# A mixer stage and a feed-forward stage that multiply before their RMSNorm is finished

## What is computed

```python
def rmsnorm(x, g):
    y = x32 * lax.rsqrt(jnp.mean(x32 * x32, axis=-1, keepdims=True) + EPS)
    return (y * g.astype(jnp.float32)).astype(x.dtype)
def modulate(h, shift, scale):
    return h * (1.0 + scale[:, None, :]) + shift[:, None, :]
...
h = modulate(rmsnorm(x, norm_g[l, 0]), sh1, sc1)
x = x + 0.5 * g1[:, None, :] * swiglu(h, w_ffn1_in[l], w_ffn1_out[l])
h = modulate(rmsnorm(x, norm_g[l, 1]), sh2, sc2)
hq, hf_f, hf_b, hi, hg, aq, ak, av = split_columns(h @ w_mix_in[l])
...
x = x + g2[:, None, :] * mixed
h = modulate(rmsnorm(x, norm_g[l, 2]), sh3, sc3)
x = x + 0.5 * g3[:, None, :] * swiglu(h, w_ffn2_in[l], w_ffn2_out[l])
```

## Time and profile before

| | us |
|---|---|
| median of 3 runs (1137.01 to 1138.49) | 1138.09 |
| the profiled execution's own time | 1136.99 |
| its span, first to last instruction | 1135.2 |
| PE busy | 1089.5 (96% of the span) |
| DVE busy | 535.4 (47%) |
| ACT busy | 417.4 (37%) |
| POOL busy | 2.9 (0%) |

### The profile page before, as it was taken

How to read it: one execution, slowest core, us unless ns; L and a number is a source line. 1 busy time by engine, 2 the same in 40 slices (tenths; PEclk the granted TensorE clock), 3 DMA queues, 4 the chain that set the end, 5 groups by cost and what they waited for, 6 DMA issues and landing times.

```text
span 1135.2 us, 12546 instructions
## 1 busy us (share of the span) xinstructions
PE 1089.5 (96%) x5023; PEld 879.4 (77%) x5023; DVE 535.4 (47%) x607; ACT 417.4 (37%) x498; POOL 2.9 (0%) x14
## 2 busy tenths in 40 slices
PE   7699999999999989999998999979999999999998
PEld 4488888888888878778885778758888888888886
DVE  5854545454454574335449984455223222232323
ACT  4542333333232243225247874225333243232321
POOL 0000000000000000000000000000000000000000
PEclk9899999999999989999999999899999999999999
DMA  8855554644355424222310001122332323323212
GB/s 338 298 186 182 189 202 167 220 154 180 125 209 189 133 61 137 95 74 74 111 38 1 2 1 38 37 75 75 111 100 84 111 76 109 108 78 111 79 69 74
DMA packets 89480, 133.46 MB, mean 118 GB/s; under 512 B 10569, under 2 KB 73413, under 8 KB 89318
## 3 DMA queue, kind: packets, MB, share of 16 engines
q1 hardware_dynamic: 89208, 130.82, 33.7%
q10 hardware_dynamic: 238, 2.17, 0.5%
HBM read 128.78 MB, written 4.19 MB: 117 GB/s over the span
## 4 chain that ended last, share of the span: by engine, by line
PE 88%; DVE 6%; ACT 3%; issue 2%; SPq 0%; DMA 0%; POOL 0%; ACTq 0%; DVEq 0%; POOLq 0%
PE bank L1191 27%; PE bank L1193 26%; PE bank L1192 26%; PE bank L1499 1%; PE bank L1229 1%; PE bank L1254 1%; DVE a_diag L1099 1%; DVE qp_both L1082 1%; DVE rinv L854 1%; DVE z L1082 1%; PE bank L1482 1%; PE bank L1217 1%; ACT kc L704 0%; PE bank L1536 0%; DVE lg L1057 0%
## 5 line engine op out<-in xcount | busy, mean ns | idle before, releaser
L1191 PE MATMUL bank<-h_hi,w_hi 128*128 128x512 f32 x976 | 385.2, 395 | 18.8 <-DVE h_lo L865 17.5
L1193 PE MATMUL bank<-h_hi,w_lo 128*128 128x512 f32 x976 | 382.9, 392 | 0.0
L1192 PE MATMUL bank<-h_lo,w_hi 128*128 128x512 f32 x976 | 382.9, 392 | 0.0
L789 DVE TENSOR_TENSOR w_lo<-w_raw,w_hi 128x2048 fp32r<-128x2048 f32 x83 | 190.3, 2292 | 331.0 <-ACT w_hi L524 331.0
L524 ACT ACTIVATE w_hi<-w_raw 128x2048 fp32r<-128x2048 f32 x83 | 158.9, 1915 | 459.8 <-PE bank L1193 459.8
L1191 PEld LDWEIGHTS bank<-h_hi,w_hi 128*128 128x128 f32 x976 | 185.5, 190 | 62.1 <-issue 11.8
L1193 PEld LDWEIGHTS bank<-h_hi,w_lo 128*128 128x128 f32 x976 | 185.1, 190 | 39.3
L1192 PEld LDWEIGHTS bank<-h_lo,w_hi 128*128 128x128 f32 x976 | 185.7, 190 | 38.2
L1191 PE MATMUL bank<-a_hi,w_hi 128*128 128x512 f32 x352 | 137.3, 390 | 0.0
L1193 PE MATMUL bank<-a_hi,w_lo 128*128 128x512 f32 x352 | 137.0, 389 | 0.0
L1192 PE MATMUL bank<-a_lo,w_hi 128*128 128x512 f32 x352 | 137.0, 389 | 0.0
(11 more groups left out here) (161 smaller groups left out, 755.6 us busy)
## 6 DMA issues: line engine op xcount, KB each, us to landing
w_raw<-in_w_ffn_in SPq DMA_DIRECT2D x44, 1024.0 KB, 5.1
ada<-in_w_ada SPq DMA_DIRECT2D x30, 1024.0 KB, 4.9
w_raw<-in_w_ffn_out SPq DMA_DIRECT2D x22, 1024.0 KB, 4.8
w_raw<-in_w_mix_in SPq DMA_DIRECT2D x11, 1024.0 KB, 5.0
ada_first<-in_w_ada SPq DMA_DIRECT2D x6, 1024.0 KB, 17.8
x_nat<-in_x SPq DMA_DIRECT2D x1, 2048.0 KB, 15.4
bias_shear<-rowpad ACTq DMA_DIRECT2D x1, 2048.0 KB, 9.6
w_raw<-in_w_mix_in SPq DMA_DIRECT2D x8, 256.0 KB, 4.4
```

Source lines behind the costliest of these rows:

```text
L789: ve.tensor_tensor(w_lo[n % 2][:], raw[n % 2][:], as_f32(w_hi[n % 2][:]), ALU.subtract).then_inc(wlo_done, 1)
L1191: te.matmul(out_ap, wh, xh, start=first, stop=False)
L1192: te.matmul(out_ap, wh, xl, start=False, stop=False)
L1193: return te.matmul(out_ap, wl, xh, start=False, stop=last)
```

## The change

For the norms r = 1 (in front of the mixer) and r = 2 (in front of the second block) the first stage behind the norm no longer takes `h`. It takes u = `xT * fac`, which needs only the residual. Since h = u·rinv + shift, W·h = (W·u)·rinv + W·shift: the per-token factor `rinv` and the per-output-channel bias W·shift come in when the stage's banks are evicted (`norm_evict`, `wbias`). The parts:

- ACT makes u's high part (`norm_scaled`) and the square of each updated tile; DVE makes u's low part (`norm_ulo`). PE's new `stage_u` waits for `ulo` tile by tile. In it, behind four of eight channel tiles, stands one `ones` matmul for the sum of squares.
- POOL adds up all eight squares in a chain of seven, makes every second `tmod` tile in two steps (times `fac`, times `rinv`), and forms W·shift: the raw weights times the shift (128x2048), three halving adds, and then two one-column matmuls on PE.
- The second stage behind the norm takes `h` as before, through `stage_h`, tile by tile. At the first boundary u and h share memory, so ACT's `h_hi` tile waits for PE to have used that tile of u (`used`).
- In the output projection the two halves of a stage are completed one after the other, and the first half's residual tile is updated in mid-stage (`mx_out`). Banks move: the halves of stage 46 + m go to banks 6 and 7, or 4 and 5.
- The last two modulation vectors come behind m = 1 and m = 2 as eight transposes each (`ada_sum`), in place of the sixteen one-column products in the gap. ACT loads the root's table ahead (`load_sqrt`). The first pair of the second block is taken out of its loop on ACT, DVE and SP.

```diff
+            def weight_bias(nm):
...
+                nc.gpsimd.tensor_tensor(nm.prod[:], raw[n % 2][:].rearrange("p (k m) -> p k m", k=DT), shift, ALU.mult
+                                        ).then_inc(nm.wacc, 1)
+                for i, w in enumerate((4, 2, 1)):
+                    pool.wait_ge(nm.wacc, i + 1)
+                    nc.gpsimd.tensor_tensor(nm.prod[:, 0:w, :], nm.prod[:, 0:w, :], nm.prod[:, w:2 * w, :], ALU.add
+                                            ).then_inc(nm.wacc, 1)
+            def norm_pool(nm):
+                for q in range(1, DT):
+                    pool.wait_ge(nm.sq, q + 1)
...
+                    nc.gpsimd.tensor_tensor(sq[:, d, :], sq[:, d, :], sq[:, before, :], ALU.add).then_inc(nm.acc, 1)
+                for i, q in enumerate(range(1, DT, 2)):
+                    nc.gpsimd.tensor_scalar(tmod[:, d, :], xT[:, d, :], fac[:, nm.r, d:d + 1], None, ALU.mult
+                                            ).then_inc(nm.tp, 1)
+                pool.wait_ge(nm.rinv, 1)
...
+                    nc.gpsimd.tensor_tensor(tmod[:, d, :], tmod[:, d, :], rinv[:], ALU.mult).then_inc(nm.tp, 1)
@@ ACT @@
+            def norm_scaled(nm, q):
+                a.wait_ge(x_upd[nm.r - 1], q + 1)
...
+                sc.activation(nm.u_hi[:, d, :], xT[:, d, :], ACT.Copy, scale=fac[:, nm.r, d:d + 1]).then_inc(nm.uhi, 1)
...
+                    if nm.r == 1 and q < DT - 1:
+                        a.wait_ge(nm.used, q + 1)
+                    elif nm.r == 1:
+                        a.wait_ge(stage_done, N_MIXIN + 1)
...
             ffn_act(ffns[0], False)
-            norm_stats(norms[1])
+            load_sqrt()
+            for q in range(DT):
+                norm_u(norms[1], q)
+            whi(N_MIXIN + 1)
+            norm_root(norms[1])
             norm_hi(norms[1])
-            whi(N_MIXIN + 1)
@@ DVE @@
+            def norm_ulo(nm, q):
+                v.wait_ge(nm.uhi, q + 1)
+                d = nm.order[q]
+                ve.scalar_tensor_tensor(nm.u_lo[:, d, :], xT[:, d, :], fac[:, nm.r, d:d + 1],
+                                        as_f32(nm.u_hi[:, d, :]), ALU.mult, ALU.subtract).then_inc(nm.ulo, 1)
             def norm_dve(nm):
                 norm_root(nm)
+                norm_t(nm, nm.order[0])
+                norm_t(nm, nm.order[2])
+                for q in range(DT):
+                    norm_lo(nm, q)
+                    if q % 2 and q + 3 < DT:
+                        norm_t(nm, nm.order[q + 3])
+            def norm_evict(nm, outs):
+                v.wait_ge(nm.wsum, 1)
+                ve.tensor_copy(wbias[:, nm.r - 1, :], nm.wbank[:, 0:2]).then_inc(nm.ev, 1)
+                for cc in range(2):
+                    ve.tensor_tensor(outs[cc], bank[cc][:], rinv[:], ALU.mult).then_inc(nm.ev, 1)
...
             for m in range(M_MIXOUT):
+                for cc in range(2):
+                    d = 2 * m + cc
+                    if cc == 0:
+                        v.wait_ge(mx_out, m + 1)
+                    else:
+                        v.wait_ge(stage_done, N_MIXOUT + m + 1)
+                    ve.scalar_tensor_tensor(xT[:, d, :], bank[6 - 2 * (m % 2) + cc][:], gates[:, 1, d:d + 1],
+                                            xT[:, d, :], ALU.mult, ALU.add).then_inc(x_upd[1], 1)
+                    if m == M_MIXOUT - 1:
+                        norm_ulo(norms[2], d)
@@ PE @@
+            def stage_u(s, banks, nm):
+                for q, k in enumerate(nm.order):
+                    pe.wait_ge(nm.ulo, q + 1)
+                    for cc in range(2):
+                        col = k * 2 * P + cc * P
+                        ins = three(banks[cc][:], w_hi[s][:, col:col + P], w_lo[s][:, col:col + P],
+                                    nm.u_hi[:, k, :], nm.u_lo[:, k, :], q == 0, q == DT - 1)
+                    if nm.r == 1 and q < DT - 1:
+                        ins.then_inc(nm.used, 1)
+                    if q == 3:
+                        pe.wait_ge(nm.acc, DT - 1)
+                        te.matmul(nm.bank[:], ones[:], sq[:, nm.order[DT - 1], :], start=True, stop=True
+                                  ).then_inc(nm.ss, 1)
+                ins.then_inc(stage_done, 1)
+                pe.wait_ge(nm.wacc, 4)
+                for cc in range(2):
+                    ins = te.matmul(nm.wbank[:, cc:cc + 1], nm.prod[:, 0, cc * P:(cc + 1) * P], ones[:, 0:1],
+                                    start=True, stop=True)
+                ins.then_inc(nm.wsum, 1)
...
+                if m == 0:
+                    stage_u(n % 2, banks, norms[1])
+                elif m == 1:
+                    pe.wait_ge(x_upd[0], DT)
+                    stage_h(n % 2, banks, norms[1])
+                    ada_sum(7, ada_acc2[:, 0], 6)
+                else:
+                    stage_k8(n % 2, banks)
```

More of the change, by code:

```diff
@@ L589, in silu @@
                     sc.activation(sil[:, 1, :], bank[1][:], ACT.Silu).then_inc(f.silu, 1)
-                with a.Fori(0, FPAIRS - 1) as i:
+                first = 0
+                if f.r:
+                    nm, first = norms[f.r], 1
+                    whi(f.n0 + 2, 0)
+                    for cc in range(2):
+                        a.wait_ge(nm.ev, cc + 2)
+                        ins = sc.activation(sil[:, cc, :], sil[:, cc, :], ACT.Silu, bias=wbias[:, 1, cc:cc + 1])
+                    ins.then_inc(f.silu, 1)
+                    whi(f.n0 + 3, 0)
+                with a.Fori(first, FPAIRS - 1) as i:
                     whi(f.n0 + 2, 2 * i)
@@ L1193, in three, with stage_k8 @@
                 return te.matmul(out_ap, wl, xh, start=False, stop=last)
[L1195 to L1206 removed]
+            def stage_k8(s, banks):
+                for cc in range(2):
+                    for k in range(DT):
+                        col = k * 2 * P + cc * P
+                        ins = three(banks[cc][:], w_hi[s][:, col:col + P], w_lo[s][:, col:col + P],
+                                    h_hi[:, k, :], h_lo[:, k, :], k == 0, k == DT - 1)
+                ins.then_inc(stage_done, 1)
@@ L1311, in out_stage @@
                             ins.then_inc(f.out, 1)
-                        if last and q >= 3:
+                        if last and q >= 3 and between:
                             between(q - 3)
@@ L1320, in ffn_pe @@
                 out_stage(FPAIRS - 1, 0, last=True)
[L1321 to L1330 removed]
+                if between:
+                    for q in range(DT - 3, DT):
+                        between(q)
+            ffn_pe(ffns[0], True, None)
+            pe.wait_ge(x_upd[0], 6)
             for m in range(M_MIXIN):
@@ L1356, in _ @@
                     pe.wait_ge(av_cp, 1)
+                    pe.wait_ge(ada_out, 9)
                     if m == 5:
@@ L1513, in _, with out_part @@
             ins.then_inc(oh_ss, 1)
-            def out_part(m, tiles):
+            def out_part(m, tiles, halves=range(2)):
                 s = (N_MIXOUT + m) % 2
-                for cc in range(2):
+                for cc in halves:
                     for k in tiles:
```

269 lines of the change are left out of this document (157 added, 112 removed).

## The result

| | before | changed |
|---|---|---|
| median of the runs, us | 1138.11 (1137.01 to 1138.49) | 1129.65 (1127.93 to 1130.75) |
| span of the profiled execution | 1135.2 | 1126.1 |
| DVE busy | 535.4 | 561.0 |
| ACT busy | 417.4 | 400.4 |
| POOL busy | 2.9 | 75.6 |

What follows compares the result with a forecast made beforehand. PE was taken to bound the kernel, with 88% of the chain. Gains of 9.4 us at the first boundary and 10.8 at the second sum to 20.2, taking 1136.99 to 1116.8, as a median 1118, range 1115.5 to 1133.5.

Steps and rivals of the forecast that it cites:

- stage 33 would follow stage 32 at once: First boundary: PE has no pause after stage 32, its half clock goes, and stage 33 ends at 422.54.
- W·shift in time: First boundary: POOL's product and halving adds take 10.2 us and end by 399, before the first square.
- POOL's add: Both boundaries: one POOL add of 128x512 taken as 1.36 us, between bounds of 0.68 and 1.36.
- The second boundary up to the reciprocal: Second boundary: stage 49 ends at 754.4, the sum starts at 759.8, the reciprocal runs 761.7 to 765.0.
- POOL's four `tmod` tiles run beside: First boundary, stage 34: PE needs no more waits, as DVE's twelve instructions take 8.0 us for 10.88 of PE.
- the case without exclusion: Both boundaries: POOL and DVE do not block each other to any weight; chance 0.50, own range 1115.5 to 1121.
- Stage 33 to stage 34: First boundary: stage 33 starts at 410.72, first `h_lo` is done at 424.1, PE waits 0.9 us from 423.1.
- Stage 34: First boundary: after the 0.9 us wait in front of it, PE needs no more waits inside this stage.
- Stage 35: First boundary: its weights come at 436.1, PE waits 0.3 us; stage 36 can start at 447.8.
- Second boundary: From the end of stage 49 to stage 53: PE waits 0.6 us before stage 51; gain 10.8 us.
- the right rival: Both boundaries: POOL blocks DVE instructions with two SBUF inputs; gain 5.1 us, time 1133 at 1.36 each; chance 0.33.
- Slower than before: Both boundaries: the same blocking with POOL instructions over 1.6 us; at 1.82 each the time is 1146; chance 0.07.

Runs made afterwards that it cites:

- experiment 2: The change with all eight `tmod` tiles on DVE, none on POOL: 1125.33 us, ratio 0.9892 to the kernel before.
- experiment 8: The changed kernel itself, run once more without an edit: 1130.27 us, ratio 0.9936 to the kernel before.
- 5: The change with the adds of squares and all `tmod` tiles on DVE, POOL keeping only W·shift: 1126.02 us, ratio 0.9896.
- 7: The change with `fac` products on ACT and POOL's `rinv` products held back until the first `h_lo` tile: 1129.54 us, ratio 0.993.
- 6: Experiment 2's kernel; at the first boundary POOL adds only five times, DVE once, PE sums two tiles: 1125.65 us, ratio 0.9897.
- 9: Experiment 2's kernel; ACT splits stage 35's weights straight behind its last `h_hi`, DVE's two small tables stand behind `w_lo`: 1124.61 us, ratio 0.9876.
- experiment 3: The change with the `fac` products on ACT, the `rinv` products staying on POOL: 1133.19 us, ratio 0.9951 to the kernel before.

## Why the prediction was wrong

**Right.** What bounds the kernel, and that stage 33 would follow stage 32 at once. W·shift in time: POOL's product took 3.60 and the whole some 11 us for 10.2. POOL's add: 1.28 alone for 1.36. The second boundary up to the reciprocal: it ends 10.6 us after stage 49 in the forecast (754.4 to 765.0) and in the trace (752.43 to 763.0).

**The step that failed** is the line "POOL's four `tmod` tiles run beside", and with it the choice of the case without exclusion, at 0.50 against 0.33. The sum used DVE's durations of a time in which POOL did nothing. Measured, by the forecast's own steps:

- *Stage 33 to stage 34*: 16.3 us (411.26 to 427.52) for a forecast of 13.4 (410.72 to 424.1). The four last low parts of u, 1.46 each, hold the weight split to 419.23 and so the reciprocal to 421.43, which is 10.2 after the start of stage 33 where the forecast had 7.7; most of the rest is the first `h_lo` (0.97 for 0.75). POOL's late sum would have held it nearly as long, as the root is through only at 421.2:

```profile
420.49 0.69 ACT L621 ACTIVATE rt<-bank,eps_t 128x512 f32<-128x512 f32 x1 [3.36 <-PE bank L1344]
```

  PE's own delays in stage 33, 1.8 of waiting for POOL's add and 1.6 of half clock (the sum and six products take 4.0 us, 2.3 at full clock in experiment 2), come out of the wait in front of stage 34: 0.2 here, 1.8 in experiment 8, where the sum ran at full clock.
- *Stage 34*: two waits inside, 3.9 together from start to start, forecast as none. The first is for POOL's product with `rinv`, which starts only at 427.68, behind four `fac` products of 2.24; the second for DVE, whose `tmod` and `h_lo` take turns with POOL at 1.77 and 1.7.
- *Stage 35*: 0.9 for 0.3. Together 7.6 late (2.9 + 3.9 + 0.6, and 0.2 in slower first products of the stages) from stage 33's start, and that start was itself 0.5 later than in the earlier trace rows.
- *Second boundary*: first pair of `tmod` and first `h_lo` 1.9 later than from DVE's old durations, then 1.8 of half clock (nine matmuls, 0.2 each): 3.7, the difference of 10.8 and 7.2.

The Trainium skill, "SBUF — State Buffer", section "Who interferes with whom", states the rule that decided: two SBUF inputs on the Vector engine against a GpSimd instruction that reads SBUF, one blocks the other. By that rule the trace agrees (w_lo 2.29 to 3.23, POOL's add 1.28 to 3.22, PSUM inputs untouched). I had it as a rival and gave it a third, since no row of before bore on it; nothing in the profile spoke against it either.

**Sized wrong within the right rival.** At 1.36 an instruction it gave gains of -1.2 and 6.3, measured 1.3 and 7.2. POOL's product with a per-channel scalar was taken as no dearer than its add; it is 1.57 alone and 2.12 in place. The wait for the sum was 1.8 instead of 3.3, the waits inside stage 34 3.4 instead of 2.0, and the largest, 5.0 in front of stage 34, measured 0.2 (1.8 in experiment 8): the products with `rinv` started only at 427.68, behind the first `h_lo` and not in front of it. The half clock, forecast as wholly gone, came back behind some of the waits: 1.6 us in stage 33, which cost nothing, and 1.8 in stage 51. So it is partly luck that the measured time lies near the rival's: terms too large and a half clock that it left out went against each other.

**Slower than before** needed a POOL instruction of over 1.6 us by itself, with exclusion on top. By itself an add takes 1.28 and a `fac` product 1.57; the 1.68 and 2.12 in place hold the turns already. At the first boundary it did come to within 1.3 us of nothing gained.

**Open.** Why half clock falls in stage 38 (at 483 to 492) in one kernel and not in another behind the same gap isn't settled by these runs. The kernel before has it too, and so have all profiled executions but those of experiments 2, 5 and 7; it moves single executions by 1 to 2 us, as much as the edits 6 and 9. What W·shift costs where it stretches DVE's instructions before the boundary wasn't tried by itself; PE did not wait there.

## What to carry to other kernels

Work moved to an idle POOL is not free for DVE: before costing it, list what DVE runs in that window, and count every DVE instruction with two SBUF inputs as taking turns with POOL, one for one (1.7 us for 0.7 in experiment 3). If POOL is used, place its instructions beside DVE work that reads PSUM, and keep them out of the few microseconds in which PE waits for DVE, with a wait if need be (about 2.4 us in the two boundaries here). After a boundary is shortened, look for the next late engine in line (here ACT's and DVE's split of stage 35) before shortening it again.

## What the runs showed of the hardware

On POOL a 128x512 product with one tile input took longer (1.57 with a per-channel scalar) than an add with two (1.28). Two engines released by the same semaphore fell into strict turns for four instructions, 1.7 us a turn (experiment 3), so that releasing POOL earlier made the kernel slower. And a wait of 1.8 us in mid-stage was followed by starts 0.43 apart in the change; in experiment 2 the same wait (418.05) was not, and the half clock came 9 us later, in stage 34. The same kernel did either: in experiment 8, the change again, it came in stage 34 too.
